# A hybrid encoder step: layer ends, first expert's rows and pool groups in another order

## The reference

```
for l in range(2):
    q, k, v, u = split(h @ w_in[l])                       # 3 * 512 + 512 columns
    a = diff_attention(q, k, v)                           # 4 heads, two softmax maps each
    p = pool_mixer(u)                                     # 4 groups of trailing means, each with its own map
    h = layer_norm(ALPHA * h + concat(a, p) @ w_out[l])
    gates = two best experts inside the best group of four, renormalised
    y = sum over 16 experts e of gates[:, e] * ((silu(h @ w_gate[l][e]) * (h @ w_up[l][e])) @ w_down[l][e])
    h = layer_norm(ALPHA * h + y)
return h of the frames, and the new keys, values and pooling inputs of each layer
```

## Time and profile before

| | before |
|---|---|
| runs, us | 1016.03, 1013.43, 1013.49 |
| median | 1013.49 |
| the profiled execution | 1016.76, span 1015.0 |
| its mean granted TensorE clock | 0.969 of full |
| busy: PE | 952.6 us (94% of the span) |
| busy: PE weight load | 788.0 us |
| busy: VectorE | 830.8 us (82%) |
| busy: ScalarE | 649.1 us |
| busy: GpSimd | 256.3 us |

### The profile page before, as it was taken

The page is one execution under the profiler, slowest core; times in us unless marked ns, Lnnn a source line. Parts: engine busy times, 40 slices in busy tenths (PEclk is TensorE's granted clock), DMA queues, the critical chain, the costliest instruction groups (busy, mean ns, idle before and its releaser), DMA issues.

```text
span 1015.0 us, 15189 instructions
## 1 busy us (share of the span) xinstructions
PE 952.6 (94%) x5102; PEld 788.0 (78%) x5102; DVE 830.8 (82%) x1213; ACT 649.1 (64%) x910; POOL 256.3 (25%) x337
## 2 busy tenths in 40 slices
PE   4999989999999999999969999898999999999992
PEld 3898868677888888888749988687888888888881
DVE  7977657679989989899884686488999898998995
ACT  4345631067888888888744456215888888888871
POOL 1433333441111111110323233335311111111021
PEclk8999989979999999999979999999999999999996
DMA  9854831389999999999983134419999999999873
GB/s 353 275 153 137 262 132 63 132 314 385 366 366 367 362 359 370 365 369 342 239 281 132 41 128 137 169 52 347 381 379 374 377 363 358 377 373 352 312 212 108
DMA packets 118318, 278.28 MB, mean 274 GB/s; under 512 B 8771, under 2 KB 11067, under 8 KB 118238
## 3 DMA queue, kind: packets, MB, share of 16 engines
q1 hardware_dynamic: 99648, 240.40, 65.8%
q0 software_dynamic: 11040, 21.14, 7.4%
q10 hardware_dynamic: 7566, 15.96, 4.5%
HBM read 266.51 MB, written 30.37 MB: 293 GB/s over the span
## 4 chain that ended last, share of the span: by engine, by line
PE 82%; DVE 9%; DMA 3%; issue 2%; ACT 2%; POOL 2%; DVEq 0%; SPq 0%; ACTq 0%; POOLq 0%
PE PS L1000 23%; PE PS L673 12%; PE PS L1005 11%; PE PS L1044 11%; PE PS L1048 6%; PE PS L985 3%; PE PS L850 2%; PE PS L851 2%; PE PS L852 2%; PE PS L1024 1%; DMA xs<-H 1%; DVE H L1635 1%; PE PS L764 1%; DVE w_lo L1288 1%; POOL D4lo L2350 1%
## 5 line engine op out<-in xcount | busy, mean ns | idle before, releaser
L1501 DVE TENSOR_TENSOR w_lo<-ring,w_hi 128x1024 fp32r<-128x1024 f32 x256 | 303.1, 1233 | 42.4 <-ACT w_hi L2035 38.8
L2035 ACT ACTIVATE w_hi<-ring 128x1024 fp32r<-128x1024 f32 x256 | 260.8, 1058 | 45.4 <-PE PS L1048 27.0
L1000 PE MATMUL PS<-w_hi,x_hi 128*128 128x512 f32 x512 | 164.2, 402 | 1.7 <-ACT x_hi L2019 1.7
L1005 PE MATMUL PS<-w_lo,x_hi 128*128 128x512 f32 x512 | 161.8, 397 | 0.2 <-DVE w_lo L1501 0.2
L1000 PE MATMUL PS<-w_hi,x_lo 128*128 128x512 f32 x512 | 160.7, 395 | 1.1 <-DVE x_lo L1491 1.1
L1508 DVE TENSOR_TENSOR w_lo<-ring,w_hi 128x1024 fp32r<-128x1024 f32 x128 | 154.4, 1220 | 4.3 <-ACT w_hi L2048 4.3
L2048 ACT ACTIVATE w_hi<-ring 128x1024 fp32r<-128x1024 f32 x128 | 135.3, 1059 | 30.3 <-PE PS L1005 28.6
L1000 PEld LDWEIGHTS PS<-w_hi,x_lo 128*128 128x128 f32 x512 | 96.7, 189 | 24.3 <-DVE x_lo L1491 1.5
L2366 POOL DMA_INDIRECT M<-xs,idx x30 | 52.2, 1740 | 249.3 <-PE PS L985 214.7
L1005 PEld LDWEIGHTS PS<-w_lo,x_hi 128*128 128x128 f32 x512 | 96.2, 188 | 23.1 <-DVE w_lo L1501 0.9
L1000 PEld LDWEIGHTS PS<-w_hi,x_hi 128*128 128x128 f32 x512 | 94.1, 189 | 22.4 <-issue 1.8
(11 more groups left out here) (276 smaller groups left out, 1613.2 us busy)
## 6 DMA issues: line engine op xcount, KB each, us to landing
ring<-in_w_gate SPq DMA_DIRECT2D x32, 2048.0 KB, 16.2
ring<-in_w_down SPq DMA_DIRECT2D x32, 2048.0 KB, 15.9
ring<-in_w_up SPq DMA_DIRECT2D x32, 2048.0 KB
ring<-in_w_in SPq DMA_DIRECT2D x8, 2048.0 KB, 17.8
ring<-in_w_out SPq DMA_DIRECT2D x4, 2048.0 KB, 8.8
ys<-H SPq DMA_DIRECT2D x2, 3072.0 KB, 20.0
H<-ys POOLq DMA_DIRECT2D x12, 512.0 KB, 8.2
M<-in_cache_k ACTq DMA_DIRECT2D x8, 512.0 KB, 3.8
```

Source lines behind the costliest of these rows:

```text
L1000: pe.matmul(PS[:, n, :], x[:, c:c + P], w_hi[j][:, k * 512:(k + 1) * 512], start=(j == 0 and k == 0 and x is x_hi[par]), stop=False)
L1005: mm = pe.matmul(PS[:, n, :], x_hi[par][:, c:c + P], lo[:, k * 512:(k + 1) * 512], start=False, stop=(j == 3 and k == 1))
L1501: dve.tensor_tensor(lo, w, w_hi[j][:, :].bitcast(F32), ALU.subtract).then_inc(up_lo, 1)
L2035: act.activation(w_hi[j][:, :], quarter(3 * par + n, j)[0], ACT.Copy).then_inc(up_hi, 1)
```

## The change

- The entry "pools" of the table of rounded parts becomes pool0, pool1 and pool2, each one group: three roundings on ScalarE, three rests on GpSimd (the third behind the head power that stood ahead of all), three waits and three groups of 6 products on TensorE.
- Router and first expert: the one-hot columns of the tile before (`made_hot`) move from `seat` into `choose`, behind the maximum of the logits. Key head 3 is turned before the last but one tile's product of first rows; `k_rows` of head 2 moves ahead of the last exponential, of head 3 behind two of the first weight roundings, and `k_stored` behind the first rows' rounding. Expert 0's rows are rounded and their rest formed in two halves, and the first gate product waits for each half by itself. The last two shares enter the combined columns on TensorE together; the index product of the last but one tile is narrow now. GpSimd stores the last rows before it does the last two shares. The first `turn_x` moves from ahead of the up product to behind two of its four quarters. `w_hi1` to `w_hi3` change places.
- End of the rounds: VectorE reads the round count before its last rest of hidden rows; `end_sum` does both halves of tile 0 first. In layer 1 VectorE's closing norm stands in the If's first body (`more < 1`), with three means first and then scale and shift in turn.
- End of layer 0: tiles 0, 1, 2 and then 3; an own sequence on VectorE with the next layer's first weight rests between; `first_two` takes 384 columns (tiles 0 to 2) as early and the 16 meta columns as late; TensorE and ScalarE have `If(more > 0)` around the further rounds alone, ahead of the closing.

The diff, cut: a hunk's number is the line before, indentation is taken off per hunk, and "..." marks lines left out.

```diff
@@ -259 @@
 x_lo = [rounded("x_lo0", "N", 3840, 1024), rounded("x_lo1", "DD", 0, 1024)]
-w_hi = [rounded(f"w_hi{i}", "QK", SUB * i, SUB) for i in range(3)] + [rounded("w_hi3", "N", 2816, SUB)]
+w_hi = [rounded(f"w_hi{i}", buf, at, SUB) for i, (buf, at) in
+        enumerate((("QK", 0), ("N", 2816), ("QK", SUB), ("QK", 2 * SUB)))]
@@ -346 @@
 seat0_done, shared = sem("seat0_done"), sem("shared")
+xt_half_ps, xt_half_hi, xt_half_lo = sem("xt_half_ps"), sem("xt_half_hi"), sem("xt_half_lo")
@@ -393 @@
-XO = {"heads01": (slice(0, 2), slice(NMETA, NTOK)), "pools": (slice(4, 7), slice(0, NTOK)),
-      "pool3": (slice(7, 8), slice(0, NTOK)), "head2": (slice(2, 3), slice(NMETA, NTOK)),
+XO = {"heads01": (slice(0, 2), slice(NMETA, NTOK)), **{f"pool{g}": (slice(4 + g, 5 + g), slice(0, NTOK)) for g in range(4)},
+      "head2": (slice(2, 3), slice(NMETA, NTOK)),
@@ -421 @@
-return (0, 1, 3, 2) if q in (0, LN2[0]) else tuple(tiles_of((q - 1) // 2))
+return (0, 1, 3, 2) if q == 0 else tuple(tiles_of((q - 1) // 2))
@@ -656 @@
-n = len(order(LN1[l])) - 1
-j = order(LN1[l])[n]
-pe.wait_ge(shared, 4 * l + n + 1)
-for k in range(2):
-    mm = pe.matmul(PS[:, 5, 0:NE], hot[k][0:TN[j], j, :], vals[0:TN[j], j, k, 2 * NE:3 * NE],
-                   start=(k == 0), stop=(k == 1))
+last = len(order(LN1[l])) - 1
+for n in (last - 1, last):
+    j = order(LN1[l])[n]
+    pe.wait_ge(shared, 4 * l + n + 1)
+    for k in range(2):
+        mm = pe.matmul(PS[:, 5, 0:NE], hot[k][0:TN[j], j, :], vals[0:TN[j], j, k, 2 * NE:3 * NE],
+                       start=(n < last and k == 0), stop=(n == last and k == 1))
@@ -679 @@
-early, late, whole = slice(0, TC[2]), slice(TC[2], NTOK), slice(0, NTOK)
+whole = slice(0, NTOK)
+if l == 0:
+    early, late = slice(0, TC[2]), slice(TC[2], NTOK)
+else:
+    early, late = slice(NMETA, NTOK), slice(0, NMETA)
...
     turn_h(l - 1, 2)
-    pe.wait_ge(comb, 3 * l)
+    pe.wait_ge(comb, 3 * l - 1)
@@ -691 @@
 term(0, hi[0], FTlo, early, stop=True)
+pe.wait_ge(wp_hi_done, 16 * l + 2)
 if l > 0:
+    term(1, hi[1], FThi, early, start=True)
...
 pe.wait_ge(ft_hi, 4 * l + 4)
-pe.wait_ge(wp_hi_done, 16 * l + 2)
-term(1, hi[1], FThi, whole, start=True)
+term(1, hi[1], FThi, late if l > 0 else whole, start=(l == 0))
@@ -863 @@
 if j == 12:
-    pe.wait_ge(xo_lo, xo_count(l, "pools"))
     pe.wait_ge(wo_lo_done, wo_count(l, 1, 3))
-    out_part(l, 0, (4, 5, 6))
+    for g in range(3):
+        pe.wait_ge(xo_lo, xo_count(l, f"pool{g}"))
+        out_part(l, 0, (4 + g,))
@@ -939 @@
                skip_group_check=True)
+if n + 1 == len(tiles) and k == KT // 2 - 1:
+    mm.then_inc(xt_half_ps, 1)
@@ -967 @@
 keys_turned(l, (2,))
+keys_turned(l, (3,))
 first_x(l, last - 1)
-keys_turned(l, (3,))
...
 pe.wait_ge(hot_done, 4 * l + last + 1)
-index_part(l, last - 1, key_bank(l) + 1, True)
+index_part(l, last - 1, key_bank(l) + 1, False)
@@ -989 @@
-def up_half(i, par, n, js):
+def up_half(i, par, n, js, by_halves=False):
...
         lo = quarter(3 * par + n, j)[1]
+        if by_halves and j == 0:
+            pe.wait_ge(xt_half_hi, l + 1)
+        if by_halves and j == 2:
+            pe.wait_ge(xt_hi, E + 1)
...
         for x in (x_hi[par], x_lo[par]):
-            if n == 0 and j == 0 and x is x_lo[par]:
+            if by_halves and j == 0 and x is x_lo[par]:
+                pe.wait_ge(xt_half_lo, l + 1)
+            elif n == 0 and j == (2 if by_halves else 0) and x is x_lo[par]:
@@ -1095 @@
 end_sum(0, 0)
+end_sum(0, 1)
 end_sum(1, 0)
-end_sum(0, 1)
@@ -1108 @@
 E = 16 * (rb + r)
-pe.wait_ge(xt_hi, E + 1)
-up_half(0, 0, 0, range(4))
+if not seated:
+    pe.wait_ge(xt_hi, E + 1)
+up_half(0, 0, 0, range(4), by_halves=seated)
+up_half(0, 0, 1, range(2))
 turn_x(0, 1)
-up_half(0, 0, 1, range(4))
+up_half(0, 0, 1, range(2, 4))
@@ -1165 @@
 R = more + 1
-with pe.If(more < 1):
-    if l + 1 < DEPTH:
-        turn_h(l, 0)
-        turn_h(l, 1)
-with pe.Else():
+with pe.If(more > 0):
@@ -1177 @@
         moe_round(l, rb, r, False)
-    if l + 1 < DEPTH:
-        turn_h(l, 0)
-        turn_h(l, 1)
+if l + 1 < DEPTH:
+    turn_h(l, 0)
+    turn_h(l, 1)
@@ -1393 @@
-def choose(l, n, offset_at):
+def choose(l, n, offset_at, placed_at):
@@ -1402 @@
 dve.tensor_reduce(negmax[p, j:j + 1], lgt[p], X, ALU.max, negate=True).then_inc(lg_max, 1)
+if n >= 1:
+    made_hot(l, n - 1, placed_at)
@@ -1430 @@
+def made_hot(l, n, placed_at):
+    j = order(LN1[l])[n]
+    p = slice(0, TN[j])
+    after(placed_at)
+    for k in range(2):
+        last = dve.tensor_scalar(hot[k][p, j, :], CT[p, C_IOTA:C_IOTA + P], place[p, j, k:k + 1], None,
+                                 ALU.is_equal)
+    last.then_inc(hot_done, 1)
@@ -1441 @@
 dve.sem_inc(rank_read, 1)
-then(dve.tensor_reduce(place[p, j, :], wide2[p], X, ALU.add))
-for k in range(2):
-    last = dve.tensor_scalar(hot[k][p, j, :], CT[p, C_IOTA:C_IOTA + P], place[p, j, k:k + 1], None,
-                             ALU.is_equal)
-last.then_inc(hot_done, 1)
+placed_at = did(dve.tensor_reduce(place[p, j, :], wide2[p], X, ALU.add))
 if n + 1 == len(order(LN1[l])):
+    made_hot(l, n, placed_at)
     then(dve.tensor_tensor(counts[p], rank, mask[p, j, :], ALU.add))
+return placed_at
@@ -1493 @@
                       ).then_inc(xt_lo, 1)
+def turned_half(half):
+    if half == 0:
+        dve.wait_ge(xt_half_hi, l + 1)
+    else:
+        dve.wait_ge(xt_hi, 16 * (rb + r) + 1)
+    c = slice(512 * half, 512 * half + 512)
+    dve.tensor_tensor(x_lo[0][:, c], PS[:, 2 + half, :], x_hi[0][:, c].bitcast(F32), ALU.subtract
+                      ).then_inc(xt_half_lo if half == 0 else xt_lo, 1)
@@ -1609 @@
-split_up(0, 0, 0, range(3))
-turned(0, 0)
 if seated:
+    split_up(0, 0, 0, range(2))
+    turned_half(0)
     partial = did(index(rb, 0, key_bank(l) + 1))
+    turned_half(1)
+    split_up(0, 0, 0, range(2, 3))
+else:
+    split_up(0, 0, 0, range(3))
+    turned(0, 0)
...
 pair(PAIRS - 1, False, True)
+if seated:
+    dve.wait_ge(routed, l + 1)
+    more = dve.value_load(more_rounds[0:1, 0:1], min_val=0, max_val=3)
...
     last_rest(1)
+    return more
@@ -1675 @@
     last.then_inc(ft_lo[l + 1], 1)
+def other_rounds(l, rb, R):
+    for n in range(len(tiles_of(l))):
+        sum_added(l, n, None).then_inc(sum_kept[l], 1)
...
+    dve.wait_ge(sum_kept[l], len(tiles_of(l)) + 1)
+def closing(l):
+    if l + 1 == DEPTH:
+        for n in range(len(tiles_of(l))):
+            mean_taken(l, n)
+        gain_at = gained(l, 0)
+        for n in range(len(tiles_of(l))):
+            shifted(l, n, gain_at)
+            if n + 1 < len(tiles_of(l)):
+                gain_at = gained(l, n + 1)
+        return
+    mean_taken(l, 0)
+    gain0 = gained(l, 0)
+    mean_taken(l, 1)
+    shifted(l, 0, gain0)
+    gain1 = gained(l, 1)
+    mean_taken(l, 2)
+    shifted(l, 1, gain1)
+    turned_rest(l, 0)
+    gain2 = gained(l, 2)
+    shifted(l, 2, gain2)
+    turned_rest(l, 1)
+    w_split(l + 1, 0)
+    turned_rest(l, 2)
+    mean_taken(l, 3)
+    w_split(l + 1, 1)
+    gain3 = gained(l, 3)
+    shifted(l, 3, gain3)
+    w_split(l + 1, 2)
+    turned_rest(l, 3)
+    w_split(l + 1, 3)
@@ -1764 @@
     offset_at = offsets(l, n)
-    if n >= 1:
-        seat(l, n - 1)
-    choose(l, n, offset_at)
+    placed_at = seat(l, n - 1) if n >= 1 else 0
+    choose(l, n, offset_at, placed_at)
 seat(l, len(tiles) - 1)
-moe_round(l, rb, 0, True)
-dve.wait_ge(routed, l + 1)
-more = dve.value_load(more_rounds[0:1, 0:1], min_val=0, max_val=3)
+more = moe_round(l, rb, 0, True)
 R = more + 1
-with dve.If(more > 0):
-    for n in range(len(tiles_of(l))):
-        sum_added(l, n, None).then_inc(sum_kept[l], 1)
...
-    dve.wait_ge(sum_kept[l], len(tiles_of(l)) + 1)
+done = steps[0]
+if l + 1 < DEPTH:
+    with dve.If(more > 0):
+        other_rounds(l, rb, R)
+    closing(l)
+else:
+    with dve.If(more < 1):
+        closing(l)
+    steps[0] = done
+    with dve.Else():
+        other_rounds(l, rb, R)
+        closing(l)
 rb = rb + R
-last = len(tiles_of(l)) - 1
-gain_at = []
-for n in range(last + 1):
-    mean_taken(l, n)
-    if n >= 1:
-        shifted(l, n - 1, gain_at[n - 1])
-    if n >= 2 and l + 1 < DEPTH:
-        turned_rest(l, n - 2)
-    gain_at.append(gained(l, n))
-if l + 1 < DEPTH:
-    w_split(l + 1, 0)
-shifted(l, last, gain_at[last])
-if l + 1 < DEPTH:
-    turned_rest(l, last - 1)
-    w_split(l + 1, 1)
-    turned_rest(l, last)
-    w_split(l + 1, 2)
-    w_split(l + 1, 3)
@@ -2020 @@
                    ).then_inc(xt_hi, 1)
+def turned_half(half):
+    if half == 0:
+        act.wait_ge(xt_half_ps, l + 1)
+    else:
+        act.wait_ge(xt_ps, E0 + 1)
+    c = slice(512 * half, 512 * half + 512)
+    act.activation(x_hi[0][:, c], PS[:, 2 + half, :], ACT.Copy
+                   ).then_inc(xt_half_hi if half == 0 else xt_hi, 1)
@@ -2113 @@
-split_up(0, 0, 0, range(3))
-turned(0, 0)
+if seated:
+    split_up(0, 0, 0, range(2))
+    k_rows(l, (3,))
+    split_up(0, 0, 0, range(2, 3))
+    turned_half(0)
+    turned_half(1)
```

(41 more changed lines are left out.)

18 lines of the change are left out of this document (9 added, 9 removed).

## The result

| | before | after |
|---|---|---|
| runs, us | 1016.03, 1013.43, 1013.49, 1016.20, 1014.78 | 1008.21, 1003.09, 1006.23, 1004.48 |
| median | 1014.78 | 1006.23 |
| profiled execution (span) | 1016.76 (1015.0) | 1008.21 (1006.4) |

The ratio is 0.9901, 95% interval 0.9877 to 0.9926: 1% faster, where 1.3% was forecast. A fifth execution of the changed kernel took 1880.52 us and is left out as disturbed. The medians differ by 8.6 us and so do the two profiled executions, so their traces can be compared stage by stage.

A forecast was written before the change was run, and what follows sets the result against it. TensorE bounds the kernel, so only its waits and slow stretches can gain. -10.4 + 0.3 - 3.5 + 0.2 gives -13.5 us unrounded: 1016.76 to 1003.3 profiled, 1000.0 as the median's like; range 994.5 to 1007.

The forecast's parts named there:

- Part 1: Output projection, both layers: pool groups in three parts end TensorE's wait and its half clock; -10.4 us, bounds -5.6 to -10.9.
- Part 2: Router and first expert: -1.4 us in layer 1, +1.7 in layer 0, -0.4 per layer from one-hot columns; together +0.3.
- Part 3: Closing norm of layer 1: early round-count read, no jump, tile 0 summed first; -3.5 us, bounds -2 to -4.
- Part 4: Closing norm of layer 0: new tile order, moved jumps, 384 columns first; +0.2 us, bounds -2 and +2.5.
- one of 16 columns will hardly be shorter: Layer 0's end: a pass of 8 products of 16 columns takes 0.95 us, against 1.00 for 128 columns.
- Step by step behind a turn at 516.3: Layer 0's closing norm: from TensorE's first turn through roundings and GpSimd's power, products start at 526.15 rather than 528.04 us.
- (a): Rival: the clock falls in the attention's tail all the same, 3.1 + 1.7 us come back, 1004.8 us; chance 0.20.
- (b): Rival: jumps at layer 0's end take longer, VectorE's +2.7 us and TensorE's +1.3, 1004.0 us; chance 0.11.
- (c): Rival: another input of the pool products is late and the waits only move, 1010.4 us; chance 0.06.
- (d): Rival: moved weight buffers slow the expert rounds' rests, 1014 us and more, slower than before; chance 0.04.

The follow-up runs named there:

- p1_alone: The kernel before with only the pool groups rounded, their rest formed and multiplied in three parts; 1007.52 us against 1016.18, ratio 0.9914.
- p3_alone: The kernel before with only the early round-count read, tile 0's sums first and layer 1's closing norm in the If's first body; 1009.55 us against 1016.18, ratio 0.9937.
- wide_late: The changed kernel with late passes over columns 0 to 143 instead of 16 and the second chunk's first product over all 400 at once; 1001.95 us, ratio 0.987.
- act_fall: The changed kernel with ScalarE's branch at layer 0's end as before, so the way of one round falls through; 1007.91 us, ratio 0.9918.

## Why the prediction was right, and where not

The gain was 8.6 us where 13.5 were forecast. Part by part:

**Part 1** (-10.4): right, step by step; alone it brought 8.7. No wait for rests, 18 products in 4.3 us, their end 5.8 us earlier in layer 0; D is 4.2 shorter without other losses (p1_alone), 4.6 forecast. Luck of the execution: before has a second half-clock stretch, 173.3 to 176.7 us, that the changed kernel lacks; it is worth about 1.2 us of the 7.7 in A and, as p3_alone and the five other kernels show, comes and goes without Part 1.

**Part 2** (+0.3): the sign in layer 0 was right and the size nearly (+1.7 forecast, with 0.4 for the one-hot columns taken off, so 2.1 for the late transposes alone; 2.2 measured by moving them back; in B it is hidden by 0.5 from the moved one-hot columns and by 6.8 us of half clock where before had 10.2). In layer 1 I forecast -1.4 and it cost 1.1. The start of the first gate product did move, but by 0.7 us in the stage instead of 2.1: the 3.4 us of half clock now lie on the last tile's first rows (the 3.64 us row at 688.74), where nothing else is waited for, and before on the tile ahead of it, which had slack. Two terms behind were mis-sized: the gather's flight, 7.1 instead of 4.42, which held TensorE's transposes by 0.2 at most, and the weight rests beside GpSimd's scaling, which took 2.0 us each where I put 1.6. The wait of 0.82 for the key copy I had put at zero, at most 0.7; it cost nothing, since behind it TensorE still waited 0.99 for the rank. The wait of 1 to 2 us ahead of the second expert's gate product came as told: 1.17, and 1.31 in layer 0.

**Part 3** (-3.5): the jump went as told. Up to the last norm step 2.2 us came in the changed kernel and 3.3 in p3_alone; what sets it is the last added rows' landing, for which I had let VectorE wait 0.9 us. It did so in p3_alone (0.89); in the changed kernel it waited 1.96. The last rows' flight was the mis-sized term, 10.2 us where 8.9 was put. That it came out at -4.2 is owed to 2.0 us behind the last store, of which the prediction says nothing. What they are stays open.

**Part 4** (+0.2): this step failed; it cost 5.1 us in C and 1.1 in D. Two terms of it. First, "one of 16 columns will hardly be shorter (0.95 taken...)": 0.92 is right at full clock, and I let the clock stay full over them. At half clock three narrow ones took 1.6 to 1.7 and the last pass over all columns 2.8 (0.92 and, in wide_late, 1.5 at full clock): 3.5 us in the changed kernel's trace. Second, "Step by step behind a turn at 516.3": the first product was to come 1.9 us sooner and came not at all, 67.8 us behind the branch before and after. I had priced TensorE's jump, which was off the path (3.52 us, under the end sums), and not ScalarE's, which the same edit moves ahead of the norm: 6.1 us, of which 0.6 to 0.9 reach TensorE. Tile 0's rows, put at 514.6, that is 54.4 us behind the branch, were ready at 57.0. By this sum VectorE's gap of 1.8, which I had put at nothing, is the larger part; no run takes it out.

The Trainium skill, "Runtime: NRT & Kernel Launch", section "Instruction fetch mechanics", says that a taken branch to code outside the two pages held stalls until its page is fetched. The trace agrees for ScalarE: 6.1 us with the jump, none with the fall-through (act_fall). My use of the rule stopped at the engine that I was watching.

**The rivals.** (a) was wrong: the clock stayed full over the pool products in both layers. (b) had a part of the truth at the wrong engine: a jump cost, but ScalarE's, and only 0.6 to 0.9 us. (c) and (d) were wrong. The result lies in the range, near its upper end: of the 6 us lost at layer 0's end, 2.0 were met by what came free behind the last store and 1.2 by the stretch that before happened to have. That it lies inside the range is in part luck.
